# Expert loop of a hybrid encoder layer: turns moved behind scatter and gather, gate loads moved ahead of up and down loads

## The reference

```python
def hier_moe(u, ...):            # top-1 of 4 groups, top-2 of its 8 experts: comb is (tokens, 32)
    for gi in range(N_GROUPS):
        hg = jnp.einsum('nd,edf->nef', t, w_gate[sl])      # 2048 -> 512
        hu = jnp.einsum('nd,edf->nef', t, w_up[sl])
        hid = jax.nn.silu(hg) * hu * comb[:, sl, None]
        out = out + jnp.einsum('nef,efd->nd', hid, w_down[sl])   # 512 -> 2048
```

## Time and profile before

| what | value |
|---|---|
| time, median of 3 runs | 1552.65 us (1552.53 to 1552.84) |
| span of the profiled execution (the only time that the page gives of it) | 1549.8 us |
| PE busy | 1521.5 us (98%) |
| DVE, ACT, POOL busy | 514.0, 222.5, 55.7 us |
| mean granted TensorE clock | 0.999 of full |
| HBM read | 476.66 MB, 309 GB/s over the span |
| expert loop | 619 to 1540 us of the span |

### The profile page before, as it was taken

How to read it: one execution, slowest core, us unless ns; L and a number is a source line. 1 busy time by engine, 2 the same in 40 slices (tenths; PEclk the granted TensorE clock), 3 DMA queues, 4 the chain that set the end, 5 groups by cost and what they waited for, 6 DMA issues and landing times.

```text
span 1549.8 us, 23417 instructions
## 1 busy us (share of the span) xinstructions
PE 1521.5 (98%) x10075; PEld 978.1 (63%) x10075; DVE 514.0 (33%) x1113; ACT 222.5 (14%) x485; POOL 55.7 (4%) x58
## 2 busy tenths in 40 slices
PE   9999999999999999999999999999999999999997
PEld 6888777778876445656556556556556556556553
DVE  2566348743583104121321321321321321321323
ACT  3002313222312203000000000000000000000003
POOL 0000121003020000000000000000000000000000
PEclk9999999999999999999999999999999999999999
DMA  9743332141236046999999999999999999999996
GB/s 349 239 160 109 110 110 88 50 166 46 89 110 272 0 175 259 380 402 420 409 430 434 432 426 435 427 430 435 432 425 434 427 431 435 432 425 430 431 430 255
DMA packets 61084, 479.60 MB, mean 309 GB/s; under 512 B 10561, under 2 KB 19282, under 8 KB 41042
## 3 DMA queue, kind: packets, MB, share of 16 engines
q1 hardware_dynamic: 60736, 478.55, 75.0%
q10 hardware_dynamic: 290, 0.23, 0.1%
HBM read 476.66 MB, written 2.10 MB: 309 GB/s over the span
## 4 chain that ended last, share of the span: by engine, by line
PE 70%; DMA 23%; DVE 4%; ACT 1%; issue 1%; POOL 0%; SPq 0%; DVEq 0%; ACTq 0%; POOLq 0%
PE bank L1094 21%; DMA ring<-in_w_up_dram 21%; PE bank L758 20%; PE bank L909 7%; PE bank L1119 7%; PE bank L1174 4%; PE bank L1052 3%; DMA ring<-in_w_down_dram 2%; DVE region_m L1729 1%; PE bank L847 1%; PE bank L827 1%; PE bank L674 1%; PE bank L850 0%; PE bank L856 0%; PE bank L1112 0%
## 5 line engine op out<-in xcount | busy, mean ns | idle before, releaser
L1094 PE MATMUL bank<-ring,region_m 128*64 128x256 f32 x4096 | 455.7, 381 | 7.0 <-DMA ring<-in_w_up_dram 7.0
L1094 PEld LDWEIGHTS bank<-ring,region_m 128*64 128x64 f32 x4096 | 290.6, 137 | 162.6 <-issue 12.6
L758 PE MATMUL bank<-region_u,ring 128*128 128x272 f32 (+2 forms) x1536 | 369.6, 393 | 0.0
L758 PEld LDWEIGHTS bank<-region_u,ring 128*128 128x128 f32 x1536 | 283.8, 190 | 52.3 <-issue 0.9
L1119 PE MATMUL bank<-region_qy,region_s 128*64 128x512 f32 x992 | 218.4, 592 | 0.5 <-issue 0.5
L1119 PEld LDWEIGHTS bank<-region_qy,region_s 128*64 128x64 f32 x992 | 71.8, 137 | 127.8 <-issue 119.1
L1964 DVE TENSOR_TENSOR region_s<-region_s,bank 128x256 f32<-128x256 f32 x32 | 13.5, 421 | 334.5 <-PE bank L1094 334.5
L1052 PEld LDWEIGHTS bank<-region_m,region_u 128*128 128x128 f32 x960 | 108.3, 192 | 11.7 <-issue 11.7
L1174 PE MATMUL bank<-region_m 128*128 128x512 f32 x256 | 114.1, 599 | 0.0
L1052 PE MATMUL bank<-region_m,region_u 128*128 128x128 f32 x960 | 111.2, 277 | 0.0
L1729 DVE SCALAR_TENSOR_TENSOR region_m<-region_qy,cols,region_m 128x256 f32<-128x256 f32 x240 | 106.7, 508 | 1.7 <-DVE region_qy L1757 0.5
(11 more groups left out here) (273 smaller groups left out, 823.0 us busy)
## 6 DMA issues: line engine op xcount, KB each, us to landing
ring<-in_w_gate_dram SPq DMA_DIRECT2D x31, 4096.0 KB, 32.7
region_qy<-in_w_down_dram SPq DMA_DIRECT2D x62, 2048.0 KB, 19.9
ring<-in_w_up_dram SPq DMA_DIRECT2D x28, 4096.0 KB, 21.8
ring<-in_w_in_dram SPq DMA_DIRECT2D x40, 1024.0 KB, 7.3
ring<-in_w_up_dram SPq DMA_DIRECT2D x8, 2048.0 KB, 10.5
ring<-in_w_out_dram SPq DMA_DIRECT2D x12, 1024.0 KB, 5.3
ring<-in_w_in_dram SPq DMA_DIRECT2D x16, 512.0 KB, 5.0
region_qy<-in_w_out_dram SPq DMA_DIRECT2D x4, 1024.0 KB, 13.0
```

The source lines that it names most:

```text
L758: last = mm(banks[n % 2][:, 0:width], slot[s][:, 512 * k + P * j:512 * k + P * (j + 1)], uT[:, 4 * g + k, T - width:T], start=g == k == 0, ...
L1094: last = mm(banks[is_up][CAP * i:CAP * (i + 1), 0:FE // 2], uTe[:, k, CAP * x_:CAP * (x_ + 1)], w[:, c0:c0 + FE // 2], start=k == 0, stop= ...
```

## The change

The gate load of the expert two ahead is issued ahead of the up load of the next expert and the down load of the current one, in the loop and in the prologue. On TensorE the turns of weights and hidden rows leave the middle of `gate_up` and stand behind the scatter, or the gather, and ahead of the gate product; in the first pair they stay. `turn_weights` waits for six adds of the scatter (bank 7 is read by then) instead of eight, and `gather` gets a wait of its own for the adds of the scatter, since banks 5 and 6 are shared.

```diff
             def stream(e, u):
+                load_gate(e, 2, u, 0)
                 load_up(e, 1, u)
                 load_d(e, 0, u)
-                load_gate(e, 2, u, 0)
+                load_gate(e, 3, u, 1)
                 load_up(e, 2, u)
                 load_d(e, 1, u)
-                load_gate(e, 3, u, 1)
...
             load_up_in_halves(1)
             load_gate(0, 3, 0, 1)
+            load_d(0, 1, 0)
             load_up_in_halves(2)
-            load_d(0, 1, 0)
+            load_gate(2, 2, 2, 0)
             load_up_in_halves(3)
             load_d(2, 0, 2)
-            load_gate(2, 2, 2, 0)
+            load_gate(2, 3, 2, 1)
             load_up_in_halves(4)
             load_d(2, 1, 2)
-            load_gate(2, 3, 2, 1)
...
                 pe.wait_ge(sel_ready, p + 1)
+                if not isinstance(p, int) or p > 1:
+
+                    pe.wait_ge(scatter_read, 8 * p - 8)
...
-                    pe.wait_ge(scatter_read, 8 * p)
+                    pe.wait_ge(scatter_read, 8 * p - 2)
...
-            def gate_up(p, x_, after_first=None, after_second=None):
+            def gate_up(p, x_, between=None):
...
-                    if quarter == 0 and after_first:
-                        after_first()
-                    if quarter == 1 and after_second:
-                        after_second()
+                    if quarter == 1 and between:
+                        between()
...
             def turns(p):
 
-                if not isinstance(p, int) or p > 0:
-
-                    pe.wait_ge(scatter_read, 8 * p)
                 pe.wait_ge(hid_ready, 2 * p + 1)
                 turn_weights(p)
                 turn_hidden(2 * p)
...
                 def between():
                     turns(p)
-                    if first_pair:
-                        if isinstance(p, int):
-
-                            pe.wait_ge(plan_ready, 1)
-                        down(p, 0)
-
-                if not first_pair:
+                    if isinstance(p, int):
+
+                        pe.wait_ge(plan_ready, 1)
+                    down(p, 0)
+
+                if first_pair:
+                    gate_up(p, 1, between)
+                else:
                     scatter(p - 1)
-                gate_up(p, 1, None, between)
-                if not first_pair:
+                    turns(p)
+                    gate_up(p, 1)
                     down(p, 0, 2 * p + 1 if last_pair else None)
                 if last_pair:
                     last_down(p, r)
                 else:
                     gather(p + 1)
-                    gate_up(p + 1, 0, lambda: pe.wait_ge(hid_ready, 2 * p + 2), lambda: turn_hidden(2 * p + 1))
+                    pe.wait_ge(hid_ready, 2 * p + 2)
+                    turn_hidden(2 * p + 1)
+                    gate_up(p + 1, 0)
                     down(p, 1)
```

## The result

| | before | changed |
|---|---|---|
| median of 15 runs | 1552.53 us | 1555.53 us |
| lowest and highest | 1550.86, 1553.56 | 1553.86, 1558.71 |
| ratio of the runs (of their means) | 1 | 1.0023 (95% interval 1.0016 to 1.0030) |
| profiled execution, span | 1549.8 us | 1556.8 us |

A forecast was written before the change was run, and what follows sets the result against it. TensorE bounds the first half of the loop, the weight stream the second. +3.6 us (loads) and -1.1 (end) make +2.5: span 1552.3, time 1555.1 us; 8-in-10 range 1551.0 to 1558.2.

The forecast's parts named there:

- One more load ahead of every up load, 9.7 us, less the idle time filled: Up to up(15): +9.7 us for place, -6.2 for idle time filled, so 3.6 later; 2.0 (0 to 4.5) still lost.
- The wait at U(2): Second half of up(2) lands at about 674.7, wanted at 673.8: a wait of about 1 us, costing nothing at the end.
- Waits from U(10) at about 900, 20 or more, 0.7 each: PE waits for up weights begin near U(10), about 900 us, instead of U(16); 20 or more, some 0.7 us each.
- The first pairs over 425 GB/s: The first pairs of the expert loop show over 425 GB/s, where the earlier trace had 399 and 416.
- C: Queue runs dry in part at g(4), g(5), g(6) and on, 4.5 to 6 us lost: 1557.6 to 1559; chance 0.14.
- The queue never empty late: Late in the loop the queue holds 9.7 us at gate issues, some 12 at up issues; pace 29.22 an expert.
- The turns at nothing, up to 0.26 us an expert if TensorE were the bound: Moved turns save nothing or up to 0.26 us an expert; neither counts while the weight stream is the bound.
- c: Part of the turns' time between G and U that does not scale with the work, 0.26 us.
- rival B: The stream doesn't bind; turns and earlier gates give TensorE the whole loop: 1537 to 1545 us; chance 0.03.
- The end, -1.1: After U(30), waits at U(31) and for d(31) go, and up to 0.26 of c: -0.9 to -1.2 us.
- Rival A: In the queue, the extra gate load takes no place ahead of the up load, or is passed: 1545.4; chance 0.08.
- D: Over the whole kernel, loss and gain cancel to within a microsecond: 1552 to 1553 us; chance 0.08.

The follow-up runs named there:

- light kernel: Only the first half of the up weights loaded from expert 5 on: 1543.08 us on the kernel before, 1536.92 us on the changed kernel.
- the loads alone: The kernel before with the new order of the loads in prologue and loop, its turns where they were: 1555.46 us, ratio 1.0020.
- the switch at 22: The changed kernel with its loop back to the old order of loads (up, down, gate) from expert 22 on: 1548.79 us, ratio 0.9982.
- the light pair: The kernel before with half the up weights loaded from expert 5 on, without and with the turns moved: 1543.08 and 1533.48 us.
- the turns alone: The changed kernel with the old order of the loads, so only the turns moved: 1550.43 us, ratio 0.9994.
- the two switches: The changed kernel with its loop back to the old order of loads at expert 22 or at 10: 1548.79 and 1549.00 us.
- the gate between up and down: The changed kernel with the old prologue and, in the loop, the gate load between up and down loads: 1564.78 us, ratio 1.0092.

## Why the prediction was right

**What bounds the kernel**: confirmed. The light kernel gives the 8 us of the earlier trace rows back (8.5), and nothing done for TensorE's pace shows in the late pairs.

**One more load ahead of every up load, 9.7 us, less the idle time filled**: right in kind, 1 us short in size. g(3) lands 36.3 us after the loop's start (643.34 + 15.4), 0.5 later than before. From there up(15) takes 1051.43 - 658.7 = 392.7 us for 40 loads, 389.6 of work: 3.1 lost, where I took 2.0. The landings say where: g(4) lands at 689.6 and so three loads take 30.8 us, 1.6 lost; g(5) at 718.8, none; g(6) to g(8) lose 0.6, 0.3 and 0.6. I had put the loss at the issues of g(4), g(5) and g(6) because they find 5 us ahead, by the rows of up(5) and up(6). That step failed: these three issues lose 0.5 us in all (g(6)), and 1.5 lie in the second half of d(1), 0.3 in d(4) and 0.6 in d(5), which were issued with 11 to 12 us ahead. So that 2.0 was near the 3.1 is in part luck. With the loads alone the same order lost 1.8 up to up(15) and with the switch at 22 1.9, in the same way: 0.2 and 0.7 at g(4) to g(6), most of the rest at d(5) or d(4).

What stands beside these losses is no issue of weights. Between the landings of the two halves of d(1), 663.64 and 670.04:

```profile
q1 hardware_dynamic: 182, 2.72, 99.8%
q8 instruction: 1, 0.02, 1.1%
```

The queue named instruction moved one packet of 16 KB (0.02 MB). The other line, the queue of the loads, has the 16 DMA engines 99.8% busy, so it is the landing that came late and not the stream that stood still. In the nine full kernels 18 issues with over 7.5 us ahead lost more than 0.15 us, and each of the 18 has such a packet in flight while it was served; three in four of the issues with as much ahead and with such a packet lost less than that, and between 875 and 1490 us of the changed kernel there is no such packet and no such loss. That the packets are the cause was not tried. Of the issues with less ahead, the switch at 22 loses 0.5 us with 2.4 ahead where up(5) lost 2.1 with 2.8. How much a queue loses is not a function of what is ahead of an issue alone; the open range of 0 to 4.5 held it.

**The wait at U(2)**: 3.2 us instead of 1, since up(2) lands behind the late d(1). As forecast it costs nothing at the end while the stream binds, and in the light kernel, where it doesn't, it is the whole price.

**Waits from U(10) at about 900, 20 or more, 0.7 each**: the first full one is at U(9), 876; 24 waits, 16.8 us, of which 22 from U(9) on have 13.7, 0.6 each.

**The first pairs over 425 GB/s**: half right. Measured as far behind the loop's start as the earlier trace rows, the first pair has 430 instead of 399, the second 414 instead of 416. Up to 750 us this is also the sign that I had given for C (under 420 past 700 us); from then on it is 431.

**The queue never empty late**: the pace of 29.22 holds from 876 to 1490.

**The turns at nothing, up to 0.26 us an expert if TensorE were the bound**: the light pair measured (57.40 - 56.75) / 2 = 0.33, over the bound. I had read c off the turns' own time alone. In the chain of the changed kernel four turns take 811.45 - 811.00 = 0.45 us and two 0.23, where it was 0.61 and 0.43: 0.18 an expert. The rest is in the products, 13.96 us for G and U without a break instead of twice 7.06. The Trainium skill, TensorEngine Tiling (Array Packing), Key Properties, has a change of tiling mode drain the array; by it the move saves two changes an expert, and the trace agrees with a gain, though no run here separates the drain from the rest. In the full kernel rival B (1537 to 1545) is out, since the turns alone are at 1550.4.

**The end, -1.1**: -1.3 measured.

**Sum**: forecast +2.5. The profiled loop has +4.6 (place and idle time), +0.7 around it (g(3) lands 0.5 later), -1.3 at the end: +4.0; the medians have +3.0. The time falls into the range. Whether the case that I called the likeliest, within 0.2 per cent, came true can't be told: the ratio is 1.0023, and its interval, 1.0016 to 1.0030, holds the edge. Rival A (no place taken) is refuted by the switch, D by the halves of the change: the gain is real and the loss is larger. C, slower by a queue that loses more, is the direction in which the forecast erred, but not by C's sites.

## What to carry to other kernels

When a queue of loads is as full as the engine that it feeds, an earlier issue is no gain by itself: count the loads that stand ahead of the one that is wanted next. A load that is wanted late, moved ahead, pushes every other back by its own duration, once, and stays there until it is taken out again. In a stretch in which the queue runs dry, an early issue fills idle time, but here no run shows that this alone pays: with the new order in the prologue only, the kernel was as fast as before, and the two switches are not clear of the turns alone. Time saved on the other resource shows only before the queue takes over, or when bytes are taken away. And before a few microseconds between two profiles are explained, the granted clock of the stretch is to be compared.

## What the runs showed of the hardware that was not expected

- Turns between a gate and an up product cost 0.33 us an expert more than the same turns behind a scatter or gather, at the full granted clock (56.75 against 57.40 us a pair).
- With 4 us ahead of the up loads 29.44 us went by from one U to the next (U(15) to U(29) of the gate between up and down), 29.22 with 12 us ahead. The loss was not even: at 3.75 to 3.77 us ahead single up loads lost from 0 to 1.3 us.
- One time the queue lost 2.1 us with 2.8 us ahead of an issue, another time 0.5 us with 2.4 ahead. What tells them apart was not tried.
- Loads with over 7.5 us ahead landed late, by 0.2 to 1.5 us, only while a 16 KB packet of the instruction queue was in flight; the DMA engines were 99.8% busy meanwhile (d(1) of the changed kernel). Not tried as a cause.
- A stretch of 3.4 us at 1.2 GHz, 610 to 620 us into the span, moved the start of the expert loop by 1.7 us (621.1 instead of 619.4) in two profiles; two such stretches by 3.0 in a third, as much as the effect studied.
